# A decoder layer on one core: four embedding projections moved behind the experts, gathers with bounds, fillers for TensorE

## The chip, the cores and the metric

One core of a Trainium2 chip runs the whole layer as one program. The metric is the device time of one execution in microseconds (us), here the median of three runs. All data is float32, and the trace records each float32 matmul as two MATMUL instructions.

## What is computed

One layer for 1024 prompt rows and 64 sample rows, which make nine tiles of 128 rows (the last is half empty).

```python
h  = rmsnorm(x); q|k|v|f|u|vb|ga|gb = h @ w_in
A  = forgetting attention   # prompt: causal; sample: 8 sequences over 2048 cached keys in pages of 128
B  = chunked gating MLP
x1 = x + (sigmoid(ga) * (A @ w_up_a) + sigmoid(gb) * (B @ w_up_b)) @ w_o
x2 = x1 + moe(rmsnorm(x1))  # best of 4 groups, then top 2 of its 8 SwiGLU experts, d_ff 512
e  = rmsnorm(p @ w_ple_proj)                      # p: 256 per row, e: 1024
y  = rmsnorm(x2 + sigmoid(rmsnorm(x2) @ w_ple_gate + b) * e)
```

`e` depends on nothing but `p`, an input, so it can be computed anywhere.

## The kernel before

The program is a row of stages (`stage_front`, ..., `stage_sample_attention`, `stage_merge`, `stage_out`, `stage_route`, `stage_moe`, `stage_overflow`, `stage_final`). In a stage each engine runs its own list of instructions in the written order, and semaphores tie the lists; between stages all engines meet at a barrier. `stage_route` only defines functions; each engine runs its one at the head of `stage_moe`'s block, so there is no barrier between router and experts.

**Sample attention** (lines 1087 to 1500). A loop over eight sequences b. For each, SyncE loads 16 pages of keys in four chunks, and behind them the bias rows; VectorE turns every chunk (`turn_keys`, L1405); TensorE adds the biases (`biases`, L1235) and the scores (`scores`, L1249) and then weighs the values of the sequence before (`values_between`, L1291). GpSimd loads values when a slot is free: the chunks of b wait for the weighing of b - 1, and those of the last sequence are issued behind all others (L1196), after their page numbers are read. Between these, TensorE does pieces of the next stage's up projections (`up_piece`, L1222; bank 7), whose products VectorE takes (`merge_a`, `merge_b`, L1419 and L1425). In VectorE's list `merge_b` of piece `BETWEEN[b]` stands behind all four `turn_keys` of sequence b + 1. `AHEAD` gives b = 3 and b = 7 one more piece before their biases.

**Router** (lines 1871 to 2215). VectorE computes the choice of group and experts for all nine tiles at once (group choice, two `first_max`, the one-hot rows OH and OHS), TensorE counts with OHS (L2030 to L2033), VectorE works out each row's slot and builds the table ON_BLOCK, and six chunks of three narrow matmuls (L2041) gather the token number of every slot into `c.idx`. Four more matmuls (L2047) spread them over quarters, VectorE writes `quarter_i` (L2196), and GpSimd starts the gathers of the first two expert units (L1938). Empty slots hold 0 and so fetch row 0.

TensorE's list in the router: turn p of tiles 0 and 1, projections of tiles 0 and 1 (L2015, each with the turn of tile t + 2 behind it), the counting, projections 2 to 4, the 18 narrow matmuls, the four quarter matmuls, projections 5 to 8. ACT copies each product to SBUF, squares it in place for the sum of squares, and writes it to DRAM (`ple_rows`).

**Experts** (lines 2217 to 2403). 24 units: 16 of one expert, 8 of two that share a tile of rows (units of 64 rows each). A unit needs its gathered rows (`lay_x`, L2372, L2378), gate and up products (L2288), SiLU and multiply (`multiply`, L2390, L2395) and the down product (L2319). ACT copies y (L2350) and writes it to DRAM. The weights come through a ring of nine slots of 2 MB; load i waits for the use of load i - 9. Slot 8's first load is the first whose expert is found by the router; SyncE issues it after `perm_done` and after all nine turns of p:

```python
sp.wait_ge(perm_done, 1)
sp.wait_ge(p_tr, NT)
for i in range(FIXED, RING):
    c.load_expert(sp, i)
```

Behind the experts SyncE loads the rows and weights of the last stage (L2250, L2253), four tiles of x1 (L2534) and two of e (L2542). `stage_overflow` (for experts with more rows than their slot) does nothing here but read the count.

**Final stage** (lines 2549 to 2748). Per tile: two gathers of y (L2596), x2 in two steps (L2680, L2683), TensorE's turn (L2648), VectorE's copy (L2690), gate matmuls (L2660; `turn_x(t + 1)` between its halves), bias, sigmoid, e times its gain, x3 and y.

## Time and profile before

| what | value |
|---|---|
| median of three runs | 1858.51 us (1858.32, 1858.51, 1865.78) |
| the profiled execution | 1862.61 us |
| its span, first to last instruction | 1861.0 us |
| mean granted TensorE clock | 0.973 of full |
| TensorE busy | 1750.0 us, 94% of the span |
| VectorE / ACT / GpSimd busy | 751.9 / 317.9 / 269.6 us |
| DMA | 436.03 MB, mean 234 GB/s |

Times in the trace are us from the start of the span. An engine's busy time is that of its instructions; a bracket behind a timeline row holds the idle time before it and what released it. PE is TensorE, DVE VectorE, POOL GpSimd, SP SyncE; a q behind a name is its queue of DMA issues. The granted clock is 1.00 at 2.4 GHz and 0.50 at 1.2 GHz.

### The profile page before, as it was taken

What the parts mean: (1) busy time and instruction counts of PE and PEld (TensorE: products, weight loads), DVE (VectorE), ACT (ScalarE), POOL (GpSimd) and SP (SyncE); (2) the same over time, 40 slices, a digit from 0 to 9 for tenths busy, and PEclk for the clock granted to TensorE, in tenths of its full rate; (3) what the DMA queues carried; (4) which work ended last, traced back from release to release, by engine and by line L of the source; (5) the groups of instructions that cost most, each with busy time, mean ns of one, the idle gap of its engine ahead of it and who ended that gap; (6) DMA issues with size and microseconds to landing.
All of it is one profiled execution on the core that took longest, in us unless ns stands there. A gap on an engine that the chain in (4) does not pass through costs nothing. (4 is left out here: it accounts for less than half of the span.)

```text
span 1861.0 us, 22989 instructions
## 1 busy us (share of the span) xinstructions
PE 1750.0 (94%) x8439; PEld 887.7 (48%) x8439; DVE 751.9 (40%) x1539; ACT 317.9 (17%) x552; POOL 269.6 (14%) x390
## 2 busy tenths in 40 slices
PE   7999999999999997998799998999999999994997
PEld 4564554556566663444465455434333333431443
DVE  4201104433334454565231226444444444442565
ACT  1000001222222223322110113200000000000122
POOL 2000004200000002333100000511111211101330
PEclk9999999999999998999899998999999999997999
DMA  8012110344444629999638315799999999999441
GB/s 288 6 20 86 49 51 1 107 146 158 127 153 162 203 90 326 354 376 352 241 135 327 136 76 229 265 355 422 425 423 424 423 422 423 424 428 372 153 152 63
DMA packets 137027, 436.03 MB, mean 234 GB/s; under 512 B 25721, under 2 KB 64314, under 8 KB 124626
## 3 DMA queue, kind: packets, MB, share of 16 engines
q1 hardware_dynamic: 101026, 337.16, 47.5%
q0 software_dynamic: 20288, 66.64, 9.8%
q10 hardware_dynamic: 15600, 30.75, 4.4%
q8 instruction: 68, 1.11, 0.2%
q14 instruction: 45, 0.37, 0.1%
HBM read 378.99 MB, written 55.51 MB: 233 GB/s over the span
## 5 line engine op out<-in xcount | busy, mean ns | idle before, releaser
L2288 PE MATMUL psum<-arena 128*128 128x512 f32 (+1 forms) x1024 | 337.1, 595 | 0.0
L907 PE MATMUL psum<-arena 128*128 128x384 f32 (+1 forms) x768 | 253.6, 475 | 2.3 <-ACT arena L938 2.2
L2390 DVE TENSOR_TENSOR arena<-arena,psum 32x128 f32<-32x128 f32 x384 | 143.4, 374 | 268.3 <-PE psum L2288 250.5
L2288 PEld LDWEIGHTS psum<-arena 128*128 128x128 f32 (+1 forms) x1024 | 131.6, 163 | 203.0 <-issue 203.0
L2319 PE MATMUL psum<-arena 128*64 128x512 f32 (+1 forms) x512 | 170.4, 596 | 10.1 <-issue 6.1
L907 PEld LDWEIGHTS psum<-arena 128*128 128x128 f32 x768 | 139.8, 191 | 75.9 <-issue 5.8
L1938 POOL DMA_INDIRECT arena<-moe_in,arena x96 | 94.3, 983 | 388.2 <-DVE arena L2372 325.8
L2319 PEld LDWEIGHTS psum<-arena 128*64 128x64 f32 (+1 forms) x512 | 68.5, 163 | 112.0 <-issue 112.0
L1743 PE MATMUL psum<-arena 128*128 128x512 f32 x256 | 114.7, 604 | 1.6 <-PEq L1518 1.6
L2660 PE MATMUL psum<-arena 128*128 128x512 f32 x256 | 113.9, 603 | 1.4 <-DVE arena L2690 1.4
L322 PE MATMUL psum<-arena 128*128 128x512 f32 x256 | 111.7, 593 | 0.0
L2660 PEld LDWEIGHTS psum<-arena 128*128 128x128 f32 x256 | 48.9, 194 | 60.2 <-issue 60.2
L1187 POOL DMA_DIRECT2D arena<-in_cache_v x112 | 60.3, 538 | 117.5 <-PE psum L1291 110.7
L1743 PEld LDWEIGHTS psum<-arena 128*128 128x128 f32 x256 | 48.2, 192 | 59.0 <-issue 59.0
L1222 PE MATMUL psum<-arena 128*128 128x512 f32 x160 | 73.4, 601 | 2.6 <-DVE arena L1419 2.6
L322 PEld LDWEIGHTS psum<-arena 128*128 128x128 f32 x256 | 47.9, 190 | 57.0 <-issue 57.0
L945 ACT ACTIVATE arena<-arena 128x128 f32<-128x128 f32 (+7 forms) x64 | 49.1, 768 | 142.1 <-DVE arena L1009 80.4
L1405 DVE STREAM_TRANSPOSE arena<-arena 128x2048 f32<-128x2048 f32 x27 | 61.7, 2297 | 18.6 <-DMA arena<-in_cache_k 18.6
L2343 ACT ACTIVATE arena<-psum 128x512 f32<-128x512 f32 x24 | 14.3, 597 | 301.4 <-PE psum L2288 301.4
L382 PE MATMUL psum<-arena 128*128 128x384 f32 (+1 forms) x192 | 58.7, 468 | 1.6 <-DVE arena L528 1.6
L347 PE MATMUL psum<-arena 128*128 128x384 f32 (+1 forms) x192 | 58.8, 469 | 0.0
L636 PE MATMUL psum<-arena 128*128 128x512 f32 x128 | 56.8, 598 | 1.7 <-PEq L217 0.9
(296 smaller groups left out, 1823.2 us busy)
## 6 DMA issues: line engine op xcount, KB each, us to landing
arena<-in_w_exp_gate SPq DMA_DIRECT2D x32, 2048.0 KB, 18.8
arena<-in_w_exp_up SPq DMA_DIRECT2D x32, 2048.0 KB, 24.7
arena<-in_w_exp_down SPq DMA_DIRECT2D x32, 2048.0 KB, 25.2
arena<-in_cache_v POOLq DMA_DIRECT2D x128, 256.0 KB, 10.0
arena<-in_cache_k SPq DMA_DIRECT2D x124, 256.0 KB, 8.2
arena<-in_w_in SPq DMA_DIRECT2D x24, 1024.0 KB, 6.3
moe_out<-arena ACTq DMA_DIRECT2D x24, 512.0 KB, 10.6
arena<-in_w_in SPq DMA_DIRECT2D x5, 2048.0 KB, 19.9
```

What stands on the lines that cost most here:

```text
L322: last = mm(c.bank[4 + r % 3][:, :], hidden_tile(HT, t)[:, k, :], W[:, n + 1, k, :], start=(k == 0), stop=(k == KD - 1))
L347: last = mm(c.bank[n % 4][:, 0:CUTS[sec + 1] - CUTS[sec]], W[:, 0, k, j * P:(j + 1) * P], HT[sec][:, k, :], start=(k == 0), stop=(k == KD ...
L907: done = mm(c.bank[7][:, 0:b - a], WG[blk % 2][:, k, q * P:(q + 1) * P], HT[p // NCOL][:, k, :], start=(k == 0), stop=(k == KD - 1))
L1187: pool.dma_start(VC[:, ch, g, :], c.cache_v[bass.ds(numbers[ch][g] * P, P), :]).then_inc(v_in[ch], 16)
L1222: last = mm(c.bank[7][:, :], UP[col % 2][:, n, k, :], src[:, 4 * half:4 * half + 4, k, :], start=(k == 0), stop=(k == KF - 1))
L1405: v.transpose(keys, keys).then_inc(turned[b % 2], 1)
L1743: last = mm(c.bank[2 * (t % 2) + half][:, :], MT[:, k, t * P:(t + 1) * P], WO[:, k, half * 512:half * 512 + 512], start=(k == 0), stop=(k ...
L1938: g.indirect_dma_start(out=XG[:, u % 2, q, :], out_offset=None, in_=quarters_of_rows, in_offset=bass.IndirectOffsetOnAxis(ap=c.quarter_i[: ...
L2288: last = mm(out[rows_, :], XT[:, u % 2, k, rows_], c.ring_tile(LOAD[kind, u, r])[:, k, :], start=(k == 0), stop=(k == KD - 1))
L2319: last = mm(y_ps[rows_, cols], ACT_T[:, u % 2, k, rows_], c.ring_tile(LOAD["down", u, r])[:, k, cols], start=(k == 0), stop=(k == KF - 1))
L2390: v.tensor_tensor(ACT_T[SW * s:SW * s + SW, u % 2, :, SW * q:SW * q + SW], SG[r, cols].rearrange("p (d k) -> p k d", k=KF), up_ps[r, cols] ...
L2660: last = mm(gate_ps[t % 2][:, half * 512:half * 512 + 512], XT[:, t % 2, k, :], c.wpg[half][:, k, :], start=(k == 0), stop=(k == KD - 1))
```

## The change

1. Projections 5 to 8 (`ROUTE_P = 5`) leave the router. Their turned p is kept in SBUF (`PT_LATE`), the four projections run at the head of the final stage's list on TensorE, ACT copies and squares them there before its first x2 square, and e stays in SBUF (`E_LATE`) without the way over DRAM. The ring for the others' e has two buffers instead of three. GpSimd works out the norm in two parts.
2. The router's choice of the group's expert logits is one masked product and one reduction in place of four products and three additions.
3. The product of ON_BLOCK and token number for the second choice goes to GpSimd; TensorE waits for it before the fourth chunk.
4. Empty slots get a number beyond the table, and the gathers are given a bound, so that such rows are not fetched.
5. Behind the experts two tiles of x1 and one of e are loaded in place of four and two, the two rows come behind the weights and x1, and x1, e and the last row follow once the first x2 is half done.
6. `keep_busy` is new: n float32 matmuls of 128x512 whose result nobody reads. They stand at eight places of the sample attention and at the end of the router.

```diff
+NOWHERE = 4096
...
+def keep_busy(nc, c, bank, n):
+    for _ in range(n):
+        nc.tensor.matmul(c.bank[bank].rearrange("p (a n) -> p a n", n=P), c.before[:],
+                         c.before[:].unsqueeze(1).to_broadcast([P, 4, P]), start=True, stop=True)
...
+                if p is None:
+                    pe.wait_ge(prod_b, len(PIECES))
+                    keep_busy(nc, c, 7, 1)
...
+                else:
+                    keep_busy(nc, c, 7, 3)
...
+            keep_busy(nc, c, 7, 1)
...
+            keep_busy(nc, c, 7, 2)
...
+                if b == 1:
+                    keep_busy(nc, c, 7, 5)
+                if b in (5, 6):
+                    pe.wait_ge(prod_b, BETWEEN[b - 1] + 1)
+                    keep_busy(nc, c, 7, 4)
...
+            keep_busy(nc, c, 7, 2)
...
-                                                  (block_at, [[P, NUNIT + NOVER]], 0, 0), (tok, [[P, NT]], 0, 1)):
+                                                  (block_at, [[P, NUNIT + NOVER]], 0, 0), (tok, [[P, NT]], -NOWHERE, 1)):
...
-                g.memset(strip_no[SW * j:SW * j + SW], float(j)).then_inc(c.sel_done, 1)
+                g.memset(strip_no[SW * j:SW * j + SW], float(j + STRIPS * NOWHERE)).then_inc(c.sel_done, 1)
...
+ROUTE_P = 5
...
-    NE_BUF = 3
+    NE_BUF = 2
+    PT_LATE = view(c, T_AT + 120 + 2 * D, NT - ROUTE_P, PLE // P, P)
+    c.turned_p = lambda t: PT[:, t % 2] if t < ROUTE_P else PT_LATE[:, t - ROUTE_P]
...
-                                 in_offset=bass.IndirectOffsetOnAxis(ap=c.quarter_i[:, q, b:b + 1], axis=0)
-                                 ).then_inc(xg_in[u % 2], 16)
+                                 in_offset=bass.IndirectOffsetOnAxis(ap=c.quarter_i[:, q, b:b + 1], axis=0),
+                                 bounds_check=TOK * STRIPS - 1, oob_is_err=False).then_inc(xg_in[u % 2], 16)
...
+    def scale_e(pool, a, b):
+        g = nc.gpsimd
+        pool.wait_ge(squared, b)
+        g.tensor_scalar(c.e_rstd[:, a:b], c.e_rstd[:, a:b], 1.0 / D, EPS, ALU.mult, ALU.add).then_inc(mean_done, 1)
+        pool.wait_ge(mean_done, 1 if a == 0 else 2)
+        g.tensor_tensor(c.e_rstd[:, a:b], c.e_rstd[:, a:b], c.neghalf[:, a:b], ALU.pow).then_inc(c.e_scaled, 1)
+    c.scale_e = scale_e
...
+        pool.wait_ge(late_blocks, 1)
+        g.tensor_tensor(ON_BLOCK[:, 1], ON_BLOCK[:, 1], bcast(tok, NB), ALU.mult).then_inc(late_blocks, 1)
...
-        pool.wait_ge(squared, NT)
-        g.tensor_scalar(c.e_rstd, c.e_rstd, 1.0 / D, EPS, ALU.mult, ALU.add).then_inc(mean_done, 1)
-        pool.wait_ge(mean_done, 1)
-        g.tensor_tensor(c.e_rstd, c.e_rstd, c.neghalf[:], ALU.pow).then_inc(c.e_scaled, 1)
+        c.scale_e(pool, 0, ROUTE_P)
...
-                    last = mm(e_ps[t % 2][:, cols], PT[:, t % 2, k, :], WPP[:, k, cols], start=(k == 0),
+                    last = mm(e_ps[t % 2][:, cols], c.turned_p(t)[:, k, :], WPP[:, k, cols], start=(k == 0),
...
-        projections(range(EARLY, MID))
+        projections(range(EARLY, ROUTE_P))
...
+            if ch == NCHUNK // 2:
+                pe.wait_ge(late_blocks, 2)
...
-        projections(range(MID, NT))
+        for t in range(ROUTE_P + 2, NT):
+            turn_p(t)
+        keep_busy(nc, c, 0, 8)
...
-            if t >= 2:
+            if 2 <= t < ROUTE_P:
...
-            s.activation(PT[:, t % 2], p_ps[:, 0:PLE].rearrange("p (k n) -> p k n", n=P), ACT.Copy
+            s.activation(c.turned_p(t), p_ps[:, 0:PLE].rearrange("p (k n) -> p k n", n=P), ACT.Copy
...
-        for t in range(NT):
-            keep_e(t)
-            if t + 2 < NT:
-                keep_p(t + 2)
+        for t in range(NT - 2):
+            if t < ROUTE_P:
+                keep_e(t)
+            keep_p(t + 2)
...
-        for g in range(NG):
-            dst = ES if g == 0 else tmp8
-            tt(dst, LG[:, :, NG + g * NEG:NG + (g + 1) * NEG], oneg[:, :, g:g + 1].to_broadcast([P, NT, NEG]),
-               ALU.mult)
-            if g:
-                tt(ES, ES, tmp8, ALU.add)
+        masked = FAR.rearrange("p t (g e) -> p t g e", g=NG)
+        tt(masked, LG[:, :, NG:].rearrange("p t (g e) -> p t g e", g=NG), oneg.unsqueeze(3).to_broadcast([P, NT, NG, NEG]),
+           ALU.mult)
+        do(v.tensor_reduce(ES, masked.rearrange("p t g e -> p t e g"), AX.X, ALU.add))
...
-        for r in range(2):
-            tt(ON_BLOCK[:, r], over_tiles(block_at, NB), bcast(hi[:, r], NB), ALU.is_equal)
-            tt(ON_BLOCK[:, r], ON_BLOCK[:, r], bcast(tok, NB), ALU.mult)
+        v.tensor_tensor(ON_BLOCK[:, 1], over_tiles(block_at, NB), bcast(hi[:, 1], NB), ALU.is_equal).then_inc(late_blocks, 1)
+        tt(ON_BLOCK[:, 0], over_tiles(block_at, NB), bcast(hi[:, 0], NB), ALU.is_equal)
+        tt(ON_BLOCK[:, 0], ON_BLOCK[:, 0], bcast(tok, NB), ALU.mult)
...
-            for sem in c.e_out:
-                sp.wait_ge(sem, 16 * (NT // len(c.e_out)))
-            for row, src in zip(c.last_rows, (c.b_ple_gate, c.norm_ple_post_g, c.norm_final_g)):
-                sp.dma_start(row, src).then_inc(c.final_in, 16)
+            for j, sem in enumerate(c.e_out):
+                sp.wait_ge(sem, 16 * len(range(j, ROUTE_P, len(c.e_out))))
...
+            for row, src in zip(c.last_rows, (c.b_ple_gate, c.norm_ple_post_g)):
+                sp.dma_start(row, src).then_inc(c.final_in, 16)
...
-            for t in range(2):
-                c.load_e(sp, t)
+            c.load_e(sp, 0)
...
-                    pe.wait_ge(c.e_squared, NT)
+                    pe.wait_ge(c.e_squared, ROUTE_P)
...
-X1_FIRST = 4
+X1_FIRST = 2
...
-    c.last_rows = [view(c, T_AT + 120 + i * D, D) for i in range(3)]
+    c.last_rows = [view(c, at, D) for at in (T_AT + 120, T_AT + 120 + D, RING_HOMES[4])]
...
-    E = c.E
+    E, E_LATE = c.E, view(c, RING_HOMES[3], NT - ROUTE_P, D)
...
-            sp.wait_ge(x2_done, 1)
-            for t in range(X1_FIRST, NT):
+            sp.wait_ge(x2_part, 1)
+            c.load_x1(sp, X1_FIRST)
+            c.load_e(sp, 1)
+            c.load_x1(sp, X1_FIRST + 1)
+            sp.dma_start(final_row, c.norm_final_g).then_inc(final_row_in, 16)
+            for t in range(X1_FIRST + 2, NT):
...
-                if 1 <= t and t + 1 < NT:
+                if 1 <= t and t + 1 < ROUTE_P:
...
+            c.scale_e(pool, ROUTE_P, NT)
...
+            for t in range(ROUTE_P, NT):
+                act.wait_ge(c.proj_mm, t + 1)
+                s.activation(E_LATE[:, t - ROUTE_P, :], gate_ps[t % 2], ACT.Copy).then_inc(c.e_kept, 1)
+                s.activation(gate_ps[t % 2], gate_ps[t % 2], ACT.Square, accum_out=c.e_rstd[:, t:t + 1]).then_inc(c.e_squared, 1)
...
+            for t in range(ROUTE_P, NT):
+                if t >= ROUTE_P + 2:
+                    pe.wait_ge(c.e_squared, t - 1)
+                for half in range(2):
+                    cols = slice(half * 512, half * 512 + 512)
+                    for k in range(PLE // P):
+                        last = mm(gate_ps[t % 2][:, cols], c.turned_p(t)[:, k, :], c.WPP[:, k, cols], start=(k == 0),
+                                  stop=(k == PLE // P - 1))
+                last.then_inc(c.proj_mm, 1)
...
-            pe.wait_ge(c.final_in, 16 * 5)
+            pe.wait_ge(c.final_in, 16 * 4)
...
+                else:
+                    pe.wait_ge(c.e_squared, NT - (t + NT - 1) % 2)
...
-                dve.wait_ge(e_in[t % 2], 16 * (t // 2 + 1))
+                if t < ROUTE_P:
+                    dve.wait_ge(e_in[t % 2], 16 * (t // 2 + 1))
+                else:
+                    dve.wait_ge(c.e_kept, NT)
+                    dve.wait_ge(c.e_scaled, 2)
...
-                v.scalar_tensor_tensor(out=EP[:, t % 2, :], in0=E[:, t % 2, :], scalar=c.e_rstd[:, t:t + 1], in1=post_row,
+                rows = E[:, t % 2, :] if t < ROUTE_P else E_LATE[:, t - ROUTE_P, :]
+                v.scalar_tensor_tensor(out=EP[:, t % 2, :], in0=rows, scalar=c.e_rstd[:, t:t + 1], in1=post_row,
...
+                if t == 0:
+                    dve.wait_ge(final_row_in, 16)
...
...
```

## Rows read from the trace of the kernel before

**Rows 1.** Busy time in stretches; behind the engines granted clock, DMA share, GB/s
```profile
700.00:870.00 170.00, 144.11 (x1976) 71.82 (x1974) 94.73 (x93) 48.41 (x83) 52.60 (x98) 0.91 1.01 361
...
1181.40:1696.50 515.10, 504.93 (x1536) 199.66 (x1535) 233.13 (x454) 41.27 (x52) 86.84 (x90) 1.00 0.99 411
...
1696.50:1721.30 24.80, 2.00 (x9) 1.63 (x9) 3.97 (x4) 2.13 (x3) 5.53 (x7) 0.55 0.88 339
```

**Rows 2.** Timeline of TensorE in the sample attention
```profile
726.18 2.09 PE L1235 MATMUL psum<-arena 8*128 8x512 f32 x8 [5.09 <-ACT arena L1379]
...
857.55 2.09 PE L1235 MATMUL psum<-arena 8*128 8x512 f32 x8 [6.47 <-DMA arena<-suffix_bias]
859.57 5.80 PE L1249 MATMUL psum<-arena 32*16 32x512 f32 x128
...
888.34 4.41 PE L1249 MATMUL psum<-arena 32*16 32x512 f32 x128
...
911.70 1.94 PE L1291 MATMUL psum<-arena 128*16 128x128 f32 x64 [1.93 <-DMA arena<-in_cache_v]
...
917.16 3.61 PE L1291 MATMUL psum<-arena 128*16 128x128 f32 x64 [3.52 <-DMA arena<-in_cache_v]
```

**Rows 3.** Timelines of VectorE and GpSimd in the sample attention
```profile
855.95 2.31 DVE L1405 STREAM_TRANSPOSE arena<-arena 128x2048 f32<-128x2048 f32 x1 [5.07 <-DMA arena<-in_cache_k]
...
858.18 0.65 DVE L1425 TENSOR_TENSOR arena<-psum,arena 128x512 f32<-128x512 f32 x1
...
892.10 0.54 POOL L1196 DMA_DIRECT2D arena<-in_cache_v  x1 [8.78 <-issue]
```

**Rows 4.** Chain that ended last, through the router: start us, us, what
```profile
1137.89 3.44 PE psum L2015 x8
...
1155.15 0.58 DVE arena L2097
...
1156.37 5.71 PE psum L2041 x36
...
1164.32 6.32 PE psum L2015 x8
...
1174.51 6.87 PE psum L2015 x16
```

**Rows 5.** Timelines of VectorE, GpSimd and SyncE's queue around the first expert unit
```profile
1140.35 0.46 DVE L2134 TENSOR_TENSOR arena<-arena 128x288 f32<-128x288 f32 x1
...
1164.36 0.32 DVE L2196 TENSOR_SCALAR arena<-psum,arena 128x96 int32<-128x96 f32 x1 [2.06 <-PE psum L2047]
...
1169.58 0.95 POOL L1938 DMA_INDIRECT arena<-moe_in,arena  x1 [0.30 <-issue]
...
1172.53 2.03 DVE L2372 TENSOR_TENSOR arena<-arena 128x1024 f32<-128x1024 f32 x1 [1.63 <-DMA arena<-moe_in,arena]
1174.59 1.25 DVE L2378 STREAM_TRANSPOSE arena<-arena 128x1024 f32<-128x1024 f32 x1
...
1175.50 13.85 SPq L1864 DMA_DIRECT2D arena<-in_w_exp_gate  x2
...
1175.70 0.95 POOL L1938 DMA_INDIRECT arena<-moe_in,arena  x1 [0.30 <-issue]
...
1185.21 2.02 DVE L2372 TENSOR_TENSOR arena<-arena 128x1024 f32<-128x1024 f32 x1 [9.37 <-DMA arena<-moe_in,arena]
```

**Rows 6.** Groups of instructions on GpSimd: busy us, mean ns, idle before
```profile
L609 POOL TENSOR_TENSOR arena<-arena 128x512 f32<-128x512 f32 x9 | 11.4, 1270 | 5.9 <-DVE arena L720 5.9
```

**Rows 7.** Chain that ended last behind the experts, and a wait of SyncE's queue
```profile
1696.46 1.03 ACT arena L2350
...
1717.89 1.98 PE psum L2648 x8
...
1721.27 9.55 PE psum L2660 x16
...
SPq L2534 <- DVE arena L2683: 14.6, 1, 14.6
```

More of the change, by code:

```diff
@@ L1925, in stage_route @@
     proj_mm, squared, mean_done, e_kept = (c.sem(n) for n in ("ple_proj_mm", "e_squared", "e_mean", "e_kept"))
-    c.e_scaled, c.e_squared = c.kept_sem("e_scaled"), squared
+    c.e_scaled, c.e_squared, c.proj_mm, c.e_kept = c.kept_sem("e_scaled"), squared, proj_mm, e_kept
     e_out = c.e_out = [c.kept_sem(f"e_out{j}") for j in range(NE_BUF)]
@@ L1938, in gather_rows @@
             g.indirect_dma_start(out=XG[:, u % 2, q, :], out_offset=None, in_=quarters_of_rows,
-                                 in_offset=bass.IndirectOffsetOnAxis(ap=c.quarter_i[:, q, b:b + 1], axis=0)
-                                 ).then_inc(xg_in[u % 2], 16)
+                                 in_offset=bass.IndirectOffsetOnAxis(ap=c.quarter_i[:, q, b:b + 1], axis=0),
+                                 bounds_check=TOK * STRIPS - 1, oob_is_err=False).then_inc(xg_in[u % 2], 16)
     c.gather_rows = gather_rows
-    EARLY, MID = 2, 5
+    EARLY = 2
     ON_BLOCK = view(c, W_AT + 2 * D, 2, NT, NB)
@@ L1956, in stage_route, with over_tiles @@
     perm_done, c.idx_done = c.sem("perm_done"), c.kept_sem("idx_done")
+    late_blocks = c.sem("late_blocks")
+    def over_tiles(row, n):
+        return row.unsqueeze(1).to_broadcast([row.shape[0], NT, n])
     quarter_mm, c.quarter_done = c.sem("quarter_mm"), c.kept_sem("quarter_done")
@@ L2091, in do @@
             dve.wait_ge(step, count[0])
-        def over_tiles(row, n):
-            return row.unsqueeze(1).to_broadcast([row.shape[0], NT, n])
         def tt(out, a, b, op):
@@ L2510, in _ @@
                         i = group * GROUP + j
-                        v.tensor_scalar(idx, c.idx[:, bass.ds(i + NUNIT, 1)], 1.0, None, ALU.mult).then_inc(picked, 1)
+                        v.tensor_scalar(idx, c.idx[:, bass.ds(i + NUNIT, 1)], float(NOWHERE), float(TOK - 1), ALU.add,
+                                        ALU.min).then_inc(picked, 1)
                         dve.wait_ge(x_in, i * 16 + 16)
@@ L2523, in _ @@
                                         ALU.mult).then_inc(act_kept, 1)
-X1_FIRST = 4
+X1_FIRST = 2
 def final_weights(c):
-    x1_back = c.x1_back = [c.kept_sem(f"x1_back{j}") for j in range(2)]
+    x1_back = c.x1_back = [c.kept_sem(f"x1_back{j}") for j in range(4)]
     def load_x1(eng, t):
-        eng.dma_start(view(c, HT_AT, NT, D)[:, t, :], c.x1_d[t * P:(t + 1) * P, :]).then_inc(x1_back[t >= X1_FIRST], 16)
+        eng.dma_start(view(c, HT_AT, NT, D)[:, t, :], c.x1_d[t * P:(t + 1) * P, :]).then_inc(x1_back[max(0, min(t, X1_FIRST + 2) - X1_FIRST + 1)], 16)
     c.load_x1 = load_x1
@@ L2566, in stage_final @@
     c.y_stored = [c.kept_sem(f"y_stored{j}") for j in range(2)]
+    final_row_in = c.sem("final_row_in")
     x2_part, x2_done = c.sem("x2_part"), c.sem("x2_done")
@@ L2676, in x2 @@
                     dve.wait_ge(c.x1_back[0], 16 * X1_FIRST)
+                elif t < X1_FIRST + 2:
+                    dve.wait_ge(c.x1_back[t - X1_FIRST + 1], 16)
                 else:
-                    dve.wait_ge(c.x1_back[1], 16 * (NT - X1_FIRST))
+                    dve.wait_ge(c.x1_back[3], 16 * (NT - X1_FIRST - 2))
                 dve.wait_ge(yg_in[t % 2], 32 * (t // 2 + 1))
@@ L2734, in _ @@
             dve.wait_ge(c.e_scaled, 1)
-            dve.wait_ge(c.final_in, 16 * 5)
+            dve.wait_ge(c.final_in, 16 * 4)
             x2(1)
@@ L2785, in _ @@
                 sp.wait_ge(c.ring_in[s], 16 * len(range(s, NLOAD, RING)))
-            sp.wait_ge(c.final_in, 16 * 5)
+            sp.wait_ge(c.final_in, 16 * 4)
 INPUTS = ["x_prompt", "x_sample", "p_prompt", "p_sample", "cache_k", "cache_v", "cache_logf", "page_table",
```

## The prediction

> **What bounds the kernel now.** I read, in this order: busy time by stretch of the span, the chain that ended last, the timelines of single engines around each place that the diff touches, and the queues' waits. The one profiled execution took 1862.61 us, of which the span is 1861.0; the median of the runs is 1858.51. The sum below is a difference, so I take it from the median.
>
> The first thing to see is that TensorE sets the time almost everywhere. In the expert stage it is busy 504.93 of 515.10 us at full clock, while the DMA share is 0.99 [rows 1]: TensorE leads, and the weights only just keep up. No wait of TensorE on a weight load stands in that stage; what is gained there can only be its starting time. The sample attention is another case: between 700 and 870 us the transfers are saturated (share 1.01) and TensorE has slack [rows 1]. The third is the stretch of 24.8 us behind the experts in which TensorE does 2.0 us of work [rows 1].
>
> **The change part by part: the router.** Before, TensorE runs its last projections from 1164.32 to 1174.51 + 6.87 = 1181.38, and the experts start right behind them [rows 1, 4]. The last four tiles of nine leave. What is then late next? The first expert unit's rows. VectorE writes the row numbers at 1164.36 to 1164.68, GpSimd issues the gathers, the rows have landed by 1172.53, the multiply takes 2.03 and the transpose ends at 1174.59 + 1.25 = 1175.84 [rows 5]. So of the 17.06 us of projections only 1181.38 - 1175.84 = 5.5 us can be won here.
>
> Against that stand three costs. First, the ninth weight load (slot 8) waits for all nine turns of p. It goes out at 1175.50 [rows 5]; with the turns done before the projections' old place, it goes out some 6.5 us earlier, about 1169, when the third and fourth gathers of unit 0 are under way. The row for such a meeting is unit 1: its gathers were issued by 1176.65 beside that load and were awaited until 1185.21 [rows 5], 8.6 us, where unit 0's, issued by 1169.58 + 0.95 on quiet queues, took 2.0. Three e writes took part in that and are gone here, and only a quarter or two of the gather meets the load: I take 1.0 us, bounds 0 and 5.5 (then the whole gain is gone). Rows that nobody needs are no longer fetched; the shorter gather is in that 1.0. Second, the gather gets a bounds check. No row shows one; a gather instruction takes 0.95 us [rows 5], so the bounds are 0 and 4 x 0.95 = 3.8 for a check that doubles it. I take 0: the check replaces descriptors by a comparison. Third, the eight fillers (16 instructions, since each such f32 matmul is recorded as two) run from about 1165.9. At full clock one takes 6.87 / 16 = 0.43, at half clock twice that, 0.86; the first eight behind 1164.32 took 6.32 with the ramp in them [rows 4]; the clock rose near 1170 before. Five at 0.86 and eleven at 0.43 make 9.0 us, to 1175: they fit, and unit 0 starts warm. I put 0.3 us for the case in which the clock falls in the pause behind them (bounds 0 and 2).
>
> The shorter group choice I cost at nothing. Its result, the sum of the one-hot rows, is written at 1140.35 + 0.46 = 1140.81, while TensorE, whose second projection ran from 1137.89 for 3.44, is free at 1141.33 [rows 4, 5]. The work that hides it is these two projections, which stay. Were they gone, it would be worth the few tenths between.
>
> The product of block table and token number for the second choice goes from VectorE to GpSimd. VectorE's chain loses one instruction of 0.58 [rows 4]. GpSimd's two-input multiply of 512 elements takes 1.27 [rows 6], so this one of 396 about 1.0; TensorE needs it for the fourth of six chunks, half of 5.71 us behind the first [rows 4], and has it in time. The two engines run at once, and whether one blocks the other no row here tells: bounds -0.6 and +1.0 (VectorE stands for one whole GpSimd multiply, less the 0.58 saved is +0.4). I take 0. The Trainium skill (SBUF — State Buffer, section "Who interferes with whom") speaks against the edit: a VectorE instruction with two SBUF inputs and a GpSimd instruction that reads SBUF block each other for a whole instruction. By that rule the sum would be about 0.4 us worse; by the row alone 0.6 better.
>
> Router: -5.5 + 1.0 + 0.3 = **-4.2 us**, bounds -6.1 and +2.
>
> **The gap behind the experts.** ACT copies the last product from 1696.46; VectorE has the first x2 at 1717.89, where TensorE turns it and then starts the gate [rows 7]. When can the moved projections begin? In the final stage's block: SyncE waited there 14.6 us for that x2, so from about 1703.2 [rows 7], and TensorE enters with it. The four tiles cost 32 instructions, 13.8 us at 0.43. They start at half clock, since TensorE has stood for 6.8 us. The ramp cost 9.55 - 6.87 = 2.7 us at the gate and 6.32 - 3.44 = 2.9 in the router [rows 4, 7]; I take 2.4. So they end at 1703.2 + 16.2 = 1719.4, about 1.5 us after x2 was there. From the turn to the gate it was 3.38 us, 1.98 of them the turn at half clock [rows 7]; now 1.0 + 1.4, and the gate starts at 1721.8, a little later than before (1721.27), but at full clock: 6.87 instead of 9.55. Its first half ends at 1728.7 against 1730.82. ACT's copy and square of the last tile (about 1.02 each, as its copy of the last product [rows 7]) end at 1721.5, just in time. The change of the load order (1.0 MB of x1, 0.5 MB of e and 0.5 MB of a row leave the busy stretch, 2.1 MB or 6 us at the 339 GB/s of that stretch [rows 1]) brings x2 forward by up to 6 us, and is hidden: the projections end last. If they were shorter, it would count. Behind the first tile TensorE sets the pace and loads and copies have room. **-2.1 us**, bounds -4 (no ramp) and +9 (all at half clock: 27.5 us).
>
> **The sample attention.** Here fillers alone are added, and each is at a wait. At the second sequence (b = 1) TensorE stands 5.09 us before the bias product [rows 2]: ten instructions at 0.43 are 4.3 us and fit. They keep the clock, so bias product and scores come 2.5 us sooner (half of 2.09, and 5.80 against 4.41 as below), but transfers set the pace there; I let the keys of b = 6 land 1.2 us sooner (bounds 0 and 3).
>
> At b = 5 and 6 the filler waits for VectorE's product of the piece before. That product stands in VectorE's queue behind the turn of the very keys that the scores await: the turn runs from 855.95 for 2.31, the product from 858.18 for 0.65 [rows 3]. Before, the bias product went at 857.55 and the scores at 859.57 for 5.80 [rows 2], to 865.37. Now: 858.83 - 1.2 = 857.6, eight instructions, five of them at half clock, 5.6 us; the bias product at full clock 1.05 (half of 2.09), the scores 4.41 (the row of b = 7 [rows 2]): 868.7, 3.3 us later. Some of it comes back, since fewer transfers meet: +3.0. Bounds: -0.7 (full clock, keys 3 us sooner) and +8.2 (all at half clock). At b = 5 the same delay ends in the wait for the keys of b = 6. Behind b = 6 nothing absorbs it: the weighing releases the values' slots, GpSimd issues the last values only from 892.10 [rows 3], and TensorE stands 3.52 us for them before 917.16 [rows 2].
>
> At the end the fillers stand in waits and pay: the last weighing takes 3.61 where the same shape took 1.94 at full clock [rows 2], -1.7; and the two last fillers may spare the next stage half of a ramp of 2.7, -1.3. Together -3.0, bounds 0 and -4.3. The sample attention comes to **0 us**, bounds -5 and +8.
>
> Sum: -4.2 - 2.1 + 0 = -6.3; 1858.51 - 6.3 = **1852.2 us**. Two of the three runs of before lie 0.2 us apart, the third 7.3 above; 0.5% (9.3 us) is about what a measurement can tell from no change.
>
> **The rivals.** *All covers hold (0.27).* The gather doesn't meet the load, GpSimd's product is free, the keys land early enough that b = 6 costs nothing, and the ramps are short: -6.1 in the router, -3.8 in the gap, -3.5 in the attention = -13.4, 1845. For it speak the 5.09 and 3.52 us waits in which fillers stand; against it the order of VectorE's queue [rows 3].
> *The experts start no sooner (0.20).* The gather of unit 0 lands only with the ninth load, as unit 1's did, or the bounds check doubles GpSimd's price: -4.2 becomes about 0, total -2.1, 1856.4. The moved projections then only fill another hole.
> *The clock does not follow the short bursts (0.07), and the change is slower.* If fillers and late projections run at half clock throughout, b = 6 is 8.2 later and the end wins nothing; in the router 16 x 0.86 = 13.8 us of filler end at 1179.7, 1.7 before the old start, and cost a ramp of 2; the late projections end at 1730.7, and the gate is 9.2 late. 8.2 + 0.3 + 9.2 = +17.7, 1876. Each instruction at half clock beyond the ramps of the sum costs 0.43: from 6.3 / 0.43 = 15 of them on the change loses. For it: after 1164.32 the first eight took 6.32 [rows 4]. Against: none of the rows shows a wide burst that stays at half clock beyond 6 us. The Trainium skill (TensorE: Matmul & The Clock Gate, section "HAM oscillation — how this bites in real kernels") warns that work chopped up by DMA waits starts cold each time; rows 7 agree for one such wait.
> *The forecast (0.40)*, and 0.06 for what I don't see.
>
> **How the numbers follow.** The forecast's own range, one term at a time moved by half its bounds, is 1848 to 1857. With the second rival inside and the first in reach, 1845 to 1860.5 leaves out most of the clock rival, part of the first, and the unseen: 2 in 10. Faster by over 0.5% needs under 1849.2: nearly all of the first rival and a little of the forecast, 0.30. Slower: the clock rival and a little unseen, 0.07. The same: 0.63.
>
> **What would show it.** The experts' first matmul about 13 us behind the row-number products of TensorE (17.1 before); unit 0's multiply on VectorE waiting for its gather, not for row numbers; the ninth load issued before the fourth gather lands. In the gap: projections from 6.8 us behind the last product, PEclk 0.50 for their first 3 to 6 us, the gate's first 16 at 6.87. At b = 5 and 6: TensorE waiting on VectorE's product, not on the bias load, and scores at 4.4. Wrong it would be if the keys land much sooner, if late projections start well before 1703 or stay at half clock, or if weights are awaited in the expert stage once it starts sooner.

## The result: slower than before, outside the forecast's range

The changed kernel took 1868.83 us (median of 13 runs, 1861.77 to 1875.15), the kernel before beside it 1863.43 us (13 runs, 1858.32 to 1865.78). The ratio is 1.0029, 95% interval [1.0019, 1.0039]: 5.4 us slower, where 6.3 us faster was forecast. (The first three runs of the kernel before, from which the forecast started, had a median 5 us lower; the ratio is what counts.) That is less than 0.5%, but with thirteen runs on either side the interval leaves no doubt of the sign.

The profiled execution took 1868.11 us, its span 1866.2 against 1861.0: +5.2, so the two profiles show the difference that the runs show.

Busy time in stretches of the changed kernel, with the columns of [rows 1]; the bounds of the last two follow the same events:

```profile
700.00:870.00 170.00, 149.14 (x2005) 75.59 (x2004) 92.45 (x91) 48.70 (x84) 52.47 (x98) 0.94 1.01 358
1185.90:1703.10 517.20, 507.15 (x1536) 200.78 (x1536) 232.88 (x454) 37.87 (x47) 88.12 (x88) 1.00 0.98 405
1703.10:1728.90 25.80, 17.68 (x41) 8.05 (x41) 3.89 (x4) 9.37 (x14) 3.79 (x4) 0.80 0.70 246
```

The stretch behind the experts is now filled (17.68 us of TensorE instead of 2.00), as meant. But the expert stage begins 4.7 us later than before (1185.9 against 1181.2), and costs 2.1 more. So the place to look is the router. TensorE there:

```profile
1141.24 0.65 PE L2069 MATMUL psum<-arena,ones 128*128 128x288 f32 x2
...
1152.61 0.44 PE L2040 MATMUL psum<-ident,arena 128*128 128x128 f32 x2 [0.80 <-ACT arena L2101]
1158.97 0.54 PE L2040 MATMUL psum<-ident,arena 128*128 128x128 f32 x2 [2.48 <-ACT arena L2101]
1159.30 7.75 PE L2082 MATMUL psum<-arena 128*128 128x44 f32 x36
1170.75 8.07 PE L154 MATMUL psum<-before 128*128 128x512 f32 x16
1185.93 22.80 PE L2325 MATMUL psum<-arena 128*128 128x512 f32 x48 [7.11 <-DVE arena L2415]
```

Two waits of TensorE on ACT's copy of the turned p are new, the token-number products begin 2.9 us later than in [rows 4] and take 7.75 us instead of 5.71, and in front of the experts TensorE stands 7.11 us, where before it stood not at all. What stands behind these, on ACT, VectorE, GpSimd and SyncE's queue:

```profile
1150.23 1.02 ACT L2113 ACTIVATE arena<-psum 128x1024 f32<-128x1024 f32 x1 [6.68 <-DMA ple_rows<-arena]
1156.59 1.02 ACT L2113 ACTIVATE arena<-psum 128x1024 f32<-128x1024 f32 x1 [4.04 <-DMA ple_rows<-arena]
...
1153.68 1.70 DVE L2137 TENSOR_TENSOR arena<-arena 128x396 f32<-128x396 f32 x2
1153.84 1.11 POOL L2022 TENSOR_TENSOR arena<-arena 128x396 f32<-128x396 f32 x1 [28.41 <-DVE arena L2220]
...
1169.35 0.32 DVE L2234 TENSOR_SCALAR arena<-psum,arena 128x96 int32<-128x96 f32 x1 [2.06 <-PE psum L2088]
1174.42 21.68 SPq L1885 DMA_DIRECT2D arena<-in_w_exp_gate  x2
1175.39 1.00 POOL L1964 DMA_INDIRECT arena<-moe_in,arena  x1 [0.30 <-issue]
1182.50 2.00 DVE L2409 TENSOR_TENSOR arena<-arena 128x1024 f32<-128x1024 f32 x1 [6.87 <-DMA arena<-moe_in,arena]
```

ACT waits twice for the write of an e tile to DRAM (`ple_rows`): the ring has two places, so tile 2 waits for the write of tile 0 and tile 3 for that of tile 1. In ACT's list the copy of the next turned p stands behind, and TensorE waits for that. The two writes were issued while SyncE's loads of expert weights (2 MB each) were under way:

```profile
1135.21 0.43 SPq L1885 DMA_DIRECT2D arena<-in_w_exp_down  x1
1135.68 0.43 SPq L1885 DMA_DIRECT2D arena<-in_w_exp_up  x1
...
1138.85 0.33 ACTq L2116 DMA_DIRECT2D ple_rows<-arena  x1
...
1142.28 0.33 ACTq L2116 DMA_DIRECT2D ple_rows<-arena  x1
```

The row numbers come at 1169.35 (1164.36 before [rows 5]). Then the ninth load goes out at 1174.42, while GpSimd issues the third gather of unit 0 and with the fourth still to come; the rows are awaited until 1182.50, 6.1 us behind the end of the last issue (1176.39) where it was 2.0.

The gap behind the experts, as the chain that ended last has it:

```profile
1709.88 16.79 PE psum L2705 x32
1726.66 0.89 PE psum L2696 x8
...
1728.90 7.11 PE psum L2719 x16
```

And TensorE in the sample attention, the rows that answer to [rows 2]:

```profile
833.21 6.22 PE L154 MATMUL psum<-before 128*128 128x512 f32 x8 [10.38 <-DVE arena L1446]
...
858.55 3.70 PE L154 MATMUL psum<-before 128*128 128x512 f32 x8
862.18 1.14 PE L1243 MATMUL psum<-arena 8*128 8x512 f32 x8
863.25 4.41 PE L1257 MATMUL psum<-arena 32*16 32x512 f32 x128
...
920.75 1.94 PE L1299 MATMUL psum<-arena 128*16 128x128 f32 x64 [2.26 <-DMA arena<-in_cache_v]
...
928.13 46.68 PE L1565 MATMUL psum<-arena 128*128 128x384 f32 x144 [2.52 <-PEq L128]
985.28 15.14 PE L1764 MATMUL psum<-arena 128*128 128x512 f32 x31 [1.60 <-PEq L1539]
```

The scores of b = 6 end at 867.66 instead of 865.37; the matmuls of the next stage begin 3.2 us late and take 46.68 instead of 49.61 us; the stage after it begins at 985.28. Those two rows before:

```profile
924.96 49.61 PE L1544 MATMUL psum<-arena 128*128 128x384 f32 x144 [2.99 <-PEq L127]
985.05 15.24 PE L1743 MATMUL psum<-arena 128*128 128x512 f32 x31 [1.59 <-PEq L1518]
```

In this profile the attention's part is +0.2.

### The profile page after: what moved, and what is told of

It reads as the page before. It is cut to its first block and busy times, and to the rows that moved or that the text cites. A ratio compares the mean times of both kernels' runs of the same rounds, so it can differ in the third digit from the quotient of the medians.

```text
span 1866.2 us, 23186 instructions
## 1 busy us (share of the span) xinstructions
PE 1766.1 (95%) x8499; PEld 895.7 (48%) x8499; DVE 750.5 (40%) x1533; ACT 317.8 (17%) x552; POOL 273.7 (15%) x393
## 3 DMA queue, kind: packets, MB, share of 16 engines
q8 instruction: 68, 1.11, 0.2%
## 5 line engine op out<-in xcount | busy, mean ns | idle before, releaser
L2380 ACT ACTIVATE arena<-psum 128x512 f32<-128x512 f32 x24 | 14.3, 597 | 320.2 <-PE psum L2325 320.2
## 6 DMA issues: line engine op xcount, KB each, us to landing
arena<-in_w_in SPq DMA_DIRECT2D x5, 2048.0 KB, 19.9
```

## The experiments

Every ratio below is to the kernel before, run beside it on the same chip. "Both repairs" stands for the first two edits together. One kernel was compared twice (without the fillers at b = 5 and 6, both repairs in it) and gave 0.9923 and 0.9937, so differences of 2 or 3 us between two ratios are not told apart from none.

**Three buffers for e again** (theory: the ring of two delays the router):

```diff
-    NE_BUF = 2
+    NE_BUF = 3
-    E = [view(c, T_AT + 120 + j * D, D) for j in range(NE_BUF)]
+    E = [view(c, T_AT + 120, D), view(c, T_AT + 120 + D, D), view(c, MOE_AT, D)]
...
         pool.wait_ge(c.quarter_done, 1)
+        pool.wait_ge(e_out[2], 16)
```

> The changed kernel, but the router's ring for e has three buffers again (the third lies in the place of the first gathered rows, and GpSimd waits for its write to DRAM before the gathers). Theory A, the ring of two: ACT stood 6.7 and 4.0 us for the e writes, its copy of the turned p came late, TensorE's turn of p and behind it the token products: they ran from 1159.30 for 7.75 us instead of 1156.37 for 5.71. With three buffers these products start near 1156 at full clock, the row numbers come 5 us sooner, and the time falls by about 5 us against the changed kernel, to that of before or a little below. Theory B, the ninth weight load beside the gathers: the load moves along, the gathers still meet it, and the fall is the same 5 us minus 0 to 1; if B were all of it, row numbers would be no sooner. Theory C, the fillers of the sample attention: nothing moves, within 1 us of the changed kernel.

Ratio 0.9995 [0.9984, 1.0006]. No write of e is awaited before the token products any more, but unit 0's rows are still late. VectorE and TensorE of this kernel:

```profile
1160.98 0.32 DVE L2235 TENSOR_SCALAR arena<-psum,arena 128x96 int32<-128x96 f32 x1 [2.06 <-PE psum L2089]
1174.33 2.00 DVE L2410 TENSOR_TENSOR arena<-arena 128x1024 f32<-128x1024 f32 x1 [7.08 <-DMA arena<-moe_in,arena]
1177.75 23.58 PE L2326 MATMUL psum<-arena 128*128 128x512 f32 x48 [6.43 <-DVE arena L2416]
```

**The ninth load behind unit 0's gather** (theory: the load delays the gather):

```diff
         sp.wait_ge(p_tr, NT)
+        sp.wait_ge(xg_in[0], 16 * STRIPS)
```

> The changed kernel, but SyncE waits until unit 0's gathered rows have landed before it issues the ninth weight load. Theory B: the gathers took 6.1 us from the last issue to VectorE's multiply instead of 2.0, since they meet this load; now they take 2 to 3, and the experts start 3.5 to 4 us sooner, at about 1182 in place of 1185.9; with the clock not falling in the shorter pause up to 2 us more. Total 3.5 to 6 us under the changed kernel. Theory A: row numbers stay at 1169.4 and the total moves by less than 1. A rival to B, that skipped rows or the bounds check make the gather slow by themselves: the 6.1 us stay.

Ratio 0.9984 [0.9970, 0.9997]. The rows are there 8.16 us behind the row numbers, as before the change, and TensorE never waits for the later load. By the ratios the kernel is 8.4 us faster than the changed one, where 3.5 to 6 were expected; the two profiles show 7.6 (5.65 at the start of the experts, 1.96 in their first 48 matmuls).

**Both repairs:**

> Both edits at once. Theories A and B add: the row numbers at about 1164 and the gathered rows 2 to 3 us behind the last issue, experts from about 1176 instead of 1185.9, 9 to 11 us less than the changed kernel, and 4 to 6 less than before. If one of the two is covered by the other, only 5 to 6 us less than the changed kernel.

Ratio 0.9955 [0.9941, 0.9969]: 13.8 us less than the changed kernel and 8.4 less than before, where 9 to 11 and 4 to 6 were expected. The expert stage itself takes 515.3 us (before 515.2). ACT, VectorE, SyncE's queue and TensorE of this kernel:

```profile
1155.44 1.02 ACT L2115 ACTIVATE arena<-psum 128x1024 f32<-128x1024 f32 x1 [2.67 <-DMA ple_rows<-arena]
...
1162.61 0.32 DVE L2236 TENSOR_SCALAR arena<-psum,arena 128x96 int32<-128x96 f32 x1 [2.06 <-PE psum L2090]
1170.77 2.02 DVE L2411 TENSOR_TENSOR arena<-arena 128x1024 f32<-128x1024 f32 x1 [1.88 <-DMA arena<-moe_in,arena]
1171.74 10.68 SPq L1885 DMA_DIRECT2D arena<-in_w_exp_gate  x2
1174.21 20.84 PE L2327 MATMUL psum<-arena 128*128 128x512 f32 x48 [1.13 <-DVE arena L2417]
```

The router of all these kernels, laid side by side. A is the row of the rank product (L2030 before, L2069 in the changed kernel), from which all times are counted, since the stages before differ from run to run by a few us. All from their timelines:

| kernel | A at | row numbers | numbers to rows multiplied | experts begin | first 48 matmuls |
|---|---|---|---|---|---|
| before | 1141.38 | 22.98 | 8.17 | 39.83 | 20.76 |
| changed | 1141.24 | 28.11 | 13.15 | 44.69 | 22.80 |
| three e buffers | 1138.10 | 22.88 | 13.35 | 39.65 | 23.58 |
| load behind gather | 1143.65 | 27.44 | 8.16 | 39.04 | 20.84 |
| both repairs | 1139.85 | 22.76 | 8.16 | 34.36 | 20.84 |

Each repair mends its own column and leaves the other's within 0.7 us. In the runs they are worth 0.34% and 0.45%, 6.3 and 8.4 us, and together 0.74%, 13.8 us: within the intervals they add.

**The ring of two in the kernel before, alone:**

```diff
-    NE_BUF = 3
+    NE_BUF = 2
```

> The kernel before with one edit: the ring of e buffers has two places instead of three. It tells whether the ring alone, without any other part of the change, delays the router. Theory (the ring is a cause by itself): ACT waits some 4 to 7 us for a write of e before its third and fourth copy, the turned p and the projection behind it are late, the token-number products begin 2 to 3 us later and at half clock (7.4 to 7.8 us instead of 5.7), the row numbers come 4 to 5 us later, and the four last projections, which need the ring too, delay the experts a little more: the time is 4 to 8 us above before, ratio 1.002 to 1.004. Rival (the ring hurts only together with the changed order of turns, load and fillers): row numbers within 1 us of 1164.4, ratio within 0.001 of 1.

Ratio 1.0011 [1.0002, 1.0020], +2 us; less than I expected. The ratio alone hardly tells this from the rival (within 0.001 of 1); the row numbers do, which are more than the rival's 1 us late. ACT, TensorE and VectorE:

```profile
1149.83 1.02 ACT L2070 ACTIVATE arena<-psum 128x1024 f32<-128x1024 f32 x1 [6.33 <-DMA ple_rows<-arena]
1155.08 1.02 ACT L2070 ACTIVATE arena<-psum 128x1024 f32<-128x1024 f32 x1 [2.93 <-DMA ple_rows<-arena]
1157.73 6.57 PE L2041 MATMUL psum<-arena 128*128 128x44 f32 x36
1166.60 0.32 DVE L2196 TENSOR_SCALAR arena<-psum,arena 128x96 int32<-128x96 f32 x1 [2.06 <-PE psum L2047]
1182.24 20.76 PE L2288 MATMUL psum<-arena 128*128 128x512 f32 x48
```

The waits are the same, but here the second write landed sooner: the row numbers come 25.40 us behind A (+2.4, not +5.1), and the token products ran 6.57 us, not 7.75. In this kernel not unit 0's rows but TensorE's own list sets the start of the experts: the projection behind the row numbers also begins 2.4 us late, but takes 5.28 instead of 6.49 us, so the experts begin at +1.2. The ring alone therefore costs 2 us here by the runs. In the changed kernel, where unit 0's rows set the start, all of the 5.1 arrives there, and the runs say 6.3.

**All fillers of the sample attention in the kernel before**, nothing else of the change:

> The kernel before with nothing but the fillers of the sample attention. My sum says 0: 3 us lost at b = 6, 3 won at the end by the clock. The two traces agree (the output stage's first matmul moved by 0.2 us), so within 1.5 us of before. Rival C, the fillers cost: +3 to +5, seen as output stage 3 us later.

Ratio 1.0004 [0.9989, 1.0020], as expected: +0.7 us, with an interval of 3 us to either side.

**Without the fillers at b = 5 and 6**, once with both repairs, once in the kernel before with the other fillers:

```diff
-                if b in (5, 6):
-                    pe.wait_ge(prod_b, BETWEEN[b - 1] + 1)
-                    keep_busy(nc, c, 7, 4)
```

> The changed kernel with three e buffers and the load behind unit 0's gather, and without the fillers at the sequences b = 5 and 6 of the sample attention (eight instructions each, which wait for VectorE's product of the piece before). It tells what these two are worth. Theory (they stand on the path): with them the scores of b = 6 ended 2.3 us later than in the kernel before, without them 2 us sooner or so, of which the last values' landing lets through at most half: 0 to 2 us faster than with them, ratio to before 0.9945 to 0.9955. Rival (they keep the clock for what follows): without them bias products and scores of b = 5 and 6 run at half clock again (2.09 and 5.80 us), and the time is the same or 1 us longer.

> The kernel before with the fillers of the sample attention alone, but without those at b = 5 and 6. With all of them the ratio to before was 1.0004. Theory (the term of the forecast was a difference of two that cancel: the fillers at b = 5 and 6 cost 3 to 5 us, the others bring as much): ratio 0.9975 to 0.9985. Rival (neither does anything outside the saturated transfers): ratio 0.9995 to 1.0005, and the gain seen without the two fillers in the kernel with both repairs was something else.

With both repairs the ratio falls from 0.9955 to 0.9923 [0.9909, 0.9938]; the same kernel in a later comparison (below) gave 0.9937 [0.9920, 0.9954], so the two fillers cost 3.4 to 6 us there. In the kernel before it falls from 1.0004 to 0.9968 [0.9958, 0.9979], 6.7 us. Both times that is more than was expected (0 to 2 us, and 3 to 5). So the term 0 was a difference of two large ones. TensorE in the kernel before with all fillers:

```profile
837.54 5.76 PE L153 MATMUL psum<-before 128*128 128x512 f32 x8 [13.07 <-DVE arena L1445]
843.24 1.14 PE L1242 MATMUL psum<-arena 8*128 8x512 f32 x8
844.31 4.41 PE L1256 MATMUL psum<-arena 32*16 32x512 f32 x128
...
862.42 3.70 PE L153 MATMUL psum<-before 128*128 128x512 f32 x8
```

and without the two:

```profile
833.69 2.09 PE L1242 MATMUL psum<-arena 8*128 8x512 f32 x8 [8.02 <-DMA arena<-suffix_bias]
835.71 6.14 PE L1256 MATMUL psum<-arena 32*16 32x512 f32 x128
...
855.56 1.14 PE L1242 MATMUL psum<-arena 8*128 8x512 f32 x8
```

Without the filler the scores of b = 5 are slow (6.14) but over at 841.85; with it they are fast (4.41) and over at 848.72. The filler of 5.76 us and the wait for VectorE's product lie on the path, and the 2.7 us that bias product and scores gain don't pay for them.

**The gathers as before** (both repairs kept; no bound, empty slots fetch row 0):

```diff
-                                 bounds_check=TOK * STRIPS - 1, oob_is_err=False).then_inc(xg_in[u % 2], 16)
+                                 ).then_inc(xg_in[u % 2], 16)
...
```

(The lines left out take `NOWHERE` out of the token numbers again.)

> The changed kernel with three e buffers and the load behind unit 0's gather, and with gathers as before: no bound, and empty slots fetch row 0. It prices the bounds check and the rows that are not fetched. Theory (the check costs nothing that sets the end): the time stays within 1.5 us of the same kernel with bounds, ratio 0.9950 to 0.9965; a gather instruction of GpSimd takes 0.95 us again instead of 1.00 to 1.63, and the four of unit 0 together 0.3 to 1.2 us less. Rival (the bounds check delays unit 0): the rows land 1 us or more sooner after the row numbers and the experts begin 1 us or more sooner. Rival (skipped rows shorten the gather): the rows land later after the last issue than 1.9 us.

Ratio 0.9953 [0.9940, 0.9966] against 0.9955 with bounds. From row numbers to multiply it is 7.99 instead of 8.16 us. Check and skipped rows together are worth nothing that these runs can tell. Inside the 8 us two parts cancel: without bounds the last of the four issues ends 6.19 us behind the row numbers and the multiply starts 1.80 behind that; with bounds it is 7.05 and 1.11. The later end has two sources, the first gather starting 1.17 us behind the start of the row numbers' instruction instead of 0.61, and the four instructions together (4.97 against 4.67 us; most take 1.00 instead of 0.95, the third 1.64).

**Without the filler in the router** (both repairs kept):

```diff
-        keep_busy(nc, c, 0, 8)
```

> The changed kernel with three e buffers and the load behind unit 0's gather, and without the eight filler matmuls at the end of the router. It tells whether they keep the clock for the first expert unit. In the kernel with them TensorE stands 1.1 us behind VectorE and its first 48 matmuls of unit 0 take 20.84 us, as before the change (20.76); where it stood 7.1 us, they took 22.80. Theory (the filler pays for the clock): without it TensorE stands some 7 us before unit 0 and these matmuls take 22.8 to 23.6: 2 to 3 us longer, ratio to before 0.9966 to 0.997. Rival (the filler is worth nothing): 20.8 again, ratio 0.9955.

Ratio 0.9979 [0.9968, 0.9989], 4.5 us worse than with it, more than expected (0.9966 to 0.997). TensorE:

```profile
1179.10 22.74 PE L2326 MATMUL psum<-arena 128*128 128x512 f32 x48 [9.97 <-DVE arena L2416]
```

The experts begin 34.50 us behind A, as with the filler (34.36), and then their first 48 matmuls take 22.74 instead of 20.84. That is 1.9 us; the 4.5 of the two ratios have an interval from about 1 to 8 us, so 1.9 may be all of it. The Trainium skill (TensorE: Matmul & The Clock Gate, section "HAM oscillation — how this bites in real kernels") describes matmuls that start cold behind each wait for a transfer; these rows agree for this wait.

**Two of the four projections back into the router.** With both repairs and without the two fillers, the first x2 is ready at 1708.83 while the late projections run to 1714.97, and in the router a filler of 9.3 us stands in a hole. So the projections of tiles 5 and 6 go there:

```diff
-ROUTE_P = 5
+ROUTE_P, MID = 7, 5
+E_BUF = (0, 1, 2, 0, 1, 0, 1)
...
-        projections(range(EARLY, ROUTE_P))
+        projections(range(EARLY, MID))
...
-        for t in range(ROUTE_P + 2, NT):
-            turn_p(t)
-        keep_busy(nc, c, 0, 8)
+        projections(range(MID, ROUTE_P))
+        keep_busy(nc, c, 0, 1)
```

> The kernel with three e buffers, the load behind unit 0's gather and no fillers at b = 5 and 6, and with only two projections (tiles 7 and 8) behind the experts: those of tiles 5 and 6 go back into the router, in the place of the filler there. In the profile of the kernel with four, the first x2 is ready 6 us before the late projections end, and TensorE's filler of 9.3 us in the router is work that nobody reads. Theory (four is two too many: the late projections, not x2, set the gate's start, and the router has a hole for two): the late projections take 9 to 10 us instead of 16.2, the first gate half starts 5 to 6 us sooner, the experts start within 1 us of the same place, and the ratio to before is 0.9885 to 0.990. Rival (what goes back into the router costs there as much, by the writes of e beside the gathers and the ninth load): unit 0 starts 3 us or more later, ratio 0.991 to 0.993.

> The kernel with three e buffers, the load behind unit 0's gather and no fillers at b = 5 and 6 once more, beside the other two, so that the two projections are judged against it on the same chip: ratio to before 0.991 to 0.9935 again.

Ratio 0.9888 [0.9871, 0.9906], as expected; the kernel with four late projections beside it 0.9937 [0.9920, 0.9954], where 0.991 to 0.9935 was expected. TensorE of the first:

```profile
1161.29 6.35 PE L2054 MATMUL psum<-arena 128*128 128x512 f32 x8
...
1173.12 20.84 PE L2325 MATMUL psum<-arena 128*128 128x512 f32 x48 [0.74 <-DVE arena L2415]
...
1695.29 9.02 PE L2705 MATMUL psum<-arena 128*128 128x512 f32 x16 [6.97 <-PEq L2466]
1705.80 1.09 PE L2696 MATMUL psum<-ident,arena 128*128 128x128 f32 x8 [1.49 <-DVE arena L2744]
1708.26 7.11 PE L2719 MATMUL psum<-arena 128*128 128x512 f32 x16 [1.36 <-issue]
```

The late projections take 9.02 us, TensorE now waits 1.49 us for x2, and the first gate half still runs at full clock. It begins 19.9 us behind the last down product instead of 25.7: 5.7 us of the 9 that the ratios say, with an interval of 4 to 5 us to either side. The experts begin 34.53 us behind A, in three profiles with both repairs and the full filler 34.0 to 34.4, so the router paid at most 0.5. It is the fastest kernel of this study: 1844.58 us (median of 4 runs, 1843.01 to 1847.41) beside 1864.38 of the kernel before.

## Why the prediction was wrong, step by step

**What failed first: a line of the diff without a term.** The prediction quotes the ring of two buffers in its list of changes and gives it no cost. In [rows 4] and [rows 5] nothing waits on a write of e, and I read that as "writes are no matter"; but three places were just enough. With both repairs, where the ring has three, tile 4's copy still waits 2.67 us for the write of tile 1, but what stands behind it in ACT's list isn't needed before the row numbers. A write issued at 1138.85 lets ACT go on at 1150.23, 11.4 us later; with projections 3.65 us apart, two places can't cover that. The trace of the kernel before had the figures: its first two writes landed 10.6 and 13.2 us behind their issue.

The writes are this slow because, as it seems, they share the DMA engines with the loads of weights: the DMA share is 1.02 between 1139 and 1150. In the changed kernel the last two of these loads land at 1149.4 and 1156.3, the two writes at 1150.2 and 1156.5. The write of tile 1 lands within 0.5 us behind the last load also with three buffers (1153.6 and 1153.4), with both repairs (1155.4 and 1155.2) and with the ring of two in the kernel before (1155.1 and 1154.7). No run moved these loads, so this cause is argued from the times and not shown; holding them back, as the ninth was held back, is untried.

The price of the ring: row numbers +5.1 us, of which 2.0 are the token products' slower run (7.75 against 5.71).

**What was mis-sized: "I take 1.0 us" for the ninth load at unit 0's gathers.** The mechanism was right (the load goes out at 1174.42, before the fourth gather's issue at 1175.39), and its upper bound of 5.5 too: it cost 5.0 us (13.15 against 8.17), and with three buffers 5.2. The load went out 5.1 us behind the row numbers, much as forecast (about 1169 against 1164.4). The reason for 1.0, that only a quarter or two meets the load, doesn't hold: the multiply needs all four quarters, so it waits for the latest one, and the fourth was issued behind the load. The Trainium skill (DMA: Bandwidth & Descriptors, section "Issuing engines are not separate DMA queues") says that transfers of all issuing engines run interleaved on the same 16 DMA engines; the rows agree, gather by GpSimd and load by SyncE.

**What was left out of both: a cold start behind them.** "Unit 0 starts warm" held only without the two delays. The filler ends at 1178.8, the rows came at 1185.8, and the first 48 matmuls took 22.80 instead of 20.76: +2.0 where 0.3 stood.

The sum, by the terms of the forecast: -5.5 winnable, +5.1 ring, +5.0 load, +2.0 clock give +6.6; the two profiles show +6.7 at the start of unit 0's down product (1202.42 and 1209.16). Forecast: -4.2.

**Right: 5.5 us to be won in the router.** With both repairs the experts begin 5.5 us sooner behind A (34.36 against 39.83), unit 0's rows set the start, as said.

**Right: the group choice and the bounds check at nothing.** The rank product stands at 1141.24 (1141.38 before). GpSimd's product: the two VectorE instructions beside it took 1.70 instead of twice 0.58 [rows 4], while GpSimd's ran for 1.11. The Trainium skill (SBUF — State Buffer, section "Who interferes with whom") has the two block each other, and the trace agrees; what the block adds is about what the moved instruction saved, and row numbers come 22.76 us behind A with it, 22.98 without. The taken 0 was right. For the bounds check the 0 was right by luck: the issues end 0.9 us later and the rows land 0.7 us sooner behind them, and neither stood in the forecast's reason.

**Nearly right: the gap, -1.5 where -2.1 was forecast.** From the end of the last down product to the end of the first gate half it is 32.9 us (1703.12 to 1736.01), before 34.4 (1696.42 to 1730.82). The late projections took 16.79 (16.2 forecast), began 6.76 us behind (6.8), and the gate ran in 7.11 (6.87). With both repairs the gap gave -2.2 (32.2 us). "The projections end last" was right too, and it held the better kernel. The new load order brought the first x2 from 21.4 to 16.9 us behind the last down product, hidden behind the projections, which ended 6.7 us after it and not 1.5. I noted that a shorter set would count, and didn't ask how many projections the gap can take.

**Right as a sum by luck, wrong in its parts: the sample attention, 0.** Measured 1.0004 alone. But b = 5 and 6 cost 6.7 us (3.0 forecast) and the rest brings 6.0 (3.0). Without the two fillers the last weighing took 1.94 instead of 3.61 us and the next stage's 144 matmuls 48.35 instead of 49.61, together 2.9, the 3.0 of the forecast; no run separates what brings the other 3. "At b = 5 the same delay ends in the wait for the keys of b = 6" failed: with the fillers, and also without those two, TensorE doesn't stand before b = 6; the wait of [rows 2] has moved in front of b = 5, where nothing absorbs it.

**The rivals.** "The experts start no sooner" named the right mechanism and stopped at its slack of 5.5 us: the gather alone, without the ring, gave that (three buffers: experts at 39.65 against 39.83, ratio 0.9995). The clock rival fell: the late projections have a mean granted clock of 0.54 until 1716.0 and 1.00 from there, and the filler at b = 6 runs in 3.70 us. The range lacked a case in which two delays add beyond the slack.

**Open:** the group choice, GpSimd's product and the load order behind the experts were read from the traces and not tried by themselves. The second write of e took 14.3 us in the changed kernel (1142.28 to 1156.59) and 12.9 in the kernel before with the ring of two (1142.23 to 1155.08), and the last weight load 20.6 and 19.3 us; why that load was quicker there is open.

## What to carry to other kernels

Give every line of a diff a term, above all a buffer taken away to make room: look up how long its write takes at that place, what else is being transferred then, and how far apart its users are, for a wait that doesn't show in the trace may be covered by one place only. A gather of several pieces is as late as its latest piece, so where nobody awaits a large load yet, let it go out behind the gather (worth 8 us here). When work is moved into a hole, measure the hole against what ends it: two projections fit both holes here, four overfilled one and left a filler in the other.

## What the runs showed of the hardware

A write of a 128x1024 f32 tile (0.5 MB) to DRAM, issued while loads of weights filled the DMA engines (share 1.02 between 1139 and 1150 in the changed kernel), held its buffer for 10.6 to 15.0 us. The mean over the whole router hides that: it is 0.43 between 1100 and 1200. An indirect gather of which one quarter was issued behind the 2 MB load was there 6.1 to 6.3 us behind its last issue; with no load beside it, 1.1 us with bounds and 1.8 to 2.0 without. Most bounded gather instructions take GpSimd 1.00 us, unbounded ones 0.95. TensorE that had stood 6.4 to 10.0 us took 22.74 to 23.58 us for 48 matmuls, after 0.7 to 1.7 us 20.84.
